# Two transformer blocks on one core: nearly half of the large expert-weight loads move from SyncE's queue to ScalarE's

## The reference, cut to what matters

```
def expert_block(args):
    xb, e = args
    hb = jax.nn.silu(xb @ w1[e]) * (xb @ w3[e])
    return hb @ w2[e]
```

## Time and profile before

| | us |
|---|---|
| median of 3 runs | 1780.15 (1780.12 to 1780.4) |
| the profiled execution, its own time | 1782.1 |
| span of the profiled execution on the core | 1780.8 |
| experts of layer 0 in the span | about 135 to 563 |
| experts of layer 1 in the span | about 677 to 1105 |

### The profile page before, as it was taken

One profiled execution on the slowest core, in us unless ns is written; L12 is line 12 of the kernel. 1 busy time (PEld: TensorE's weight loads), 2 busy tenths in 40 slices (PEclk: granted clock), 3 DMA queues, 4 the chain that ended last, 5 costly groups with the idle time before them and its releaser, 6 DMA issues.

```text
span 1780.8 us, 24002 instructions
## 1 busy us (share of the span) xinstructions
PE 1715.7 (96%) x10024; PEld 1119.8 (63%) x10024; DVE 790.6 (44%) x1510; ACT 624.1 (35%) x1197; POOL 120.7 (7%) x143
## 2 busy tenths in 40 slices
PE   9999999999999989999999989999999999999998
PEld 8974344433334974444333333887999898789986
DVE  6961111111103782111111012866888677668875
ACT  5541111000003661000000002666666564756664
POOL 0000000000000000000000000131111001401100
PEclk9999999999999999999999999999999999999999
DMA  9669999999999779999999999533555544435550
GB/s 389 239 246 409 421 428 428 427 429 426 427 424 419 277 300 394 409 430 429 426 428 428 426 425 419 182 127 134 183 182 190 189 166 146 139 128 174 185 189 24
DMA packets 55940, 544.90 MB, mean 306 GB/s; under 512 B 6288, under 2 KB 6288, under 8 KB 8336
## 3 DMA queue, kind: packets, MB, share of 16 engines
q1 hardware_dynamic: 55440, 542.14, 75.6%
q10 hardware_dynamic: 384, 1.13, 0.2%
HBM read 542.19 MB, written 1.05 MB: 305 GB/s over the span
## 4 chain that ended last, share of the span: by engine, by line
PE 69%; DMA 19%; DVE 7%; ACT 3%; issue 1%; POOL 1%; SPq 0%; DVEq 0%; ACTq 0%
PE PS L1136 24%; DMA ring<-in_w 19%; PE PS L407 12%; PE PS L409 11%; PE PS L408 11%; PE PS L1116 2%; DVE wl L390 2%; PE PS L1190 1%; PE PS L858 1%; PE PS L1152 1%; PE PS L617 1%; ACT wh L384 1%; PE PS L1204 1%; PE PS L1299 0%; DVE F L993 0%
## 5 line engine op out<-in xcount | busy, mean ns | idle before, releaser
L1136 PE MATMUL PS<-ring,F 128*64 128x512 f32 x2080 | 464.8, 597 | 26.7 <-DMA ring<-in_w 21.8
L390 DVE TENSOR_TENSOR wl<-ring,wh 128x512 fp32r<-128x512 f32 x504 | 363.3, 739 | 167.1 <-ACT wh L384 164.6
L384 ACT ACTIVATE wh<-ring 128x512 fp32r<-128x512 f32 x504 | 314.6, 631 | 272.0 <-PE PS L409 258.6
L1136 PEld LDWEIGHTS PS<-ring,F 128*64 128x64 f32 x2080 | 147.2, 137 | 321.1 <-issue 283.8
L407 PE MATMUL PS<-xh,wl 128*128 128x256 f32 x1168 | 336.5, 288 | 2.4 <-DVE wl L390 2.3
L408 PE MATMUL PS<-xl,wh 128*128 128x256 f32 x1168 | 330.3, 283 | 0.0
L409 PE MATMUL PS<-xh,wh 128*128 128x256 f32 x1168 | 330.3, 283 | 0.0
L407 PEld LDWEIGHTS PS<-xh,wl 128*128 128x128 f32 x1168 | 223.9, 192 | 5.6 <-DVE wl L390 2.6
L408 PEld LDWEIGHTS PS<-xl,wh 128*128 128x128 f32 x1168 | 223.9, 192 | 0.7
L409 PEld LDWEIGHTS PS<-xh,wh 128*128 128x128 f32 x1168 | 223.9, 192 | 0.0
L407 PE MATMUL PS<-wh,xl 128*128 128x512 f32 x352 | 142.6, 405 | 6.4 <-DVE xl L524 3.4
(11 more groups left out here) (391 smaller groups left out, 1881.4 us busy)
## 6 DMA issues: line engine op xcount, KB each, us to landing
ring<-in_w SPq DMA_DIRECT2D x100, 2048.0 KB, 25.6
ring<-in_w SPq DMA_DIRECT2D x66, 1024.0 KB, 10.5
ring<-in_ffn_up SPq DMA_DIRECT2D x44, 1024.0 KB, 4.9
early<-in_w SPq DMA_DIRECT2D x16, 2048.0 KB, 27.0
F<-in_w SPq DMA_DIRECT2D x16, 2048.0 KB, 29.2
ring<-in_ffn_down SPq DMA_DIRECT2D x22, 1024.0 KB, 4.9
F<-in_w SPq DMA_DIRECT2D x21, 1024.0 KB, 8.1
ZX<-in_w SPq DMA_DIRECT2D x8, 2048.0 KB, 26.9
```

The lines of the kernel that those rows point to most:

```text
L384: act.e.activation(self.wh[:, p % NPIECE, :], self.piece_source(p), ACT.Copy).then_inc(*self.up("w_hi", p))
L390: dve.e.tensor_tensor(self.wl[:, p % NPIECE, :], self.piece_source(p), f32(self.wh[:, p % NPIECE, :]), ALU.subtract).then_inc(*self.up("w_ ...
L1136: t = pe.e.matmul(PS[64 * half:64 * half + 64, bank, :], lhs(k), weights[:, a:a + 512], start=(k == 0), stop=(k == 7))
```

## The change

`_scalar_loads` picks the double loads for ScalarE: those for which the later of the two slots' former chunks is the last quarter of a matrix (`last % 4 == 3`). That is 30 of the 70 double loads of layer 0 (chunks 44, 64, 68, 72 and so on by four to 136, then 142, 146 and so on to 178), and 31 of layer 1 (60, 64 and so on to 124, then 130, 134, 136, 138, 142, 146 and so on to 178). SyncE leaves these out. ScalarE issues each one right after its operation that follows the product which used that last quarter: after the tanh (product with w1), after the copy of the turned hidden values (w3), or after the upper half of the result (w2). The slots, the sizes, the addresses and the signals are those of before.

```
+def _scalar_loads():
+    made = {}
+    for layer in range(2):
+        m = CHUNK[f"moe{layer}"]
+        for n in range(m, m + 192):
+            if FIRST_OF[n] == n and SIZE[n] == 2 and PREVIOUS[n + 1] >= m:
+                last = max(PREVIOUS[n], PREVIOUS[n + 1]) - m
+                if last % 4 == 3:
+                    made[n] = (layer, last // 12, last // 4 % 3)
+    return made
+BY_SCALAR = _scalar_loads()
...
     def sync_load(self, first, last):
-            if FIRST_OF[n] != n:
+            if FIRST_OF[n] != n or n in BY_SCALAR:
                 continue
...
+    def scalar_loads(self, layer, ex, w):
+        act = self.act
+        for n, after in BY_SCALAR.items():
+            if after == (layer, ex, w):
+                act.wait_ge(self.released(PREVIOUS[n]), self.released(PREVIOUS[n + 1]))
+                act.e.dma_start(self.chunk(n, 2), self.source(n)).then_inc(self.ring_sems[SLOT[n]], 16)
...
     def moe_scalar(self, layer, first, last):
             act.e.activation(v["hh"], PS[:, 4, :], ACT.Tanh, scale=0.5).then_inc(*up("tanh", layer, ex))
+            self.scalar_loads(layer, ex, 0)
...
             act.e.activation(v["hT"], PS[:, 4, :], ACT.Copy).then_inc(*up("hid_t", layer, ex))
+            self.scalar_loads(layer, ex, 1)
...
             act.e.activation(v["Y"][o][0:64, :], PS[0:64, 5, :], ACT.Copy).then_inc(*up("y0", layer, ex))
+            self.scalar_loads(layer, ex, 2)
```

## The result

The changed kernel takes 1788.9 us (median of 4, 1785.87 to 1791.31) against 1780.28 us (1780.12 to 1781.84) of before on the same chip: ratio 1.0043, 95% interval 1.0031 to 1.0055, so slower; the two medians are 8.6 us apart. On another chip it took 1790.42 against 1781.1 us, ratio 1.0052 (1.0038 to 1.0065). The profiled execution took 1786.99 us with a span of 1785.7, 4.9 us over before's span. Before's profiled execution was itself 1.8 us over its median (1782.1 against 1780.28), so lateness read between two profiles comes out that much smaller than the difference of the medians.

The account below looks back on a forecast made before the run. The prediction took the DMA transfers to set the pace until TensorE is work-bound at each layer's end. Terms 0 + 0 + 0 + 3.0 + 3.2 = 6.2 us on the 1780.15 us median gave 1786.3 us, range 1776 to 1797.

Parts of the forecast that it names:

- The bound, SyncE and ScalarE: Experts of both layers: loads run at one rate throughout; SyncE's 61 fewer issues and ScalarE's 61 issues each change 0.
- The rate with two queues: Weight loads in the experts: two queues move no more than one, 0; bounds 1% less and 1.9% more.
- faster rival: Weight loads: two queues hide what one leaves between packets, as in a 436 GB/s window; 6.9 us faster, 1773.3; chance 14%.
- The order of landing: End of each layer's experts: SyncE's chunk 172 lands only when all bytes up to 175 are in; 3.0 and 3.2 us.
- so the lead persists: ScalarE's loads land early: Experts' loads: each queue gets one load in two at half rate, so ScalarE's wait in their slots and SyncE's arrive last.
- layer 1's 3.2 us: End of layer 1's experts: chunks 172 to 175 run after 1062.16 in 7.1 us against 3.65, less 0.28 of waiting.
- the upper bound's case: End of each layer: ScalarE's 178 too gets ahead of SyncE's 172, another 4.9 us, up to 7.9 us a layer.

Follow-up runs that it names:

- one_packet: Kernel before, all real loads SyncE's; ScalarE issues 61 extra 8-byte one-packet loads, each waiting only for the third before it: 1781.07 against 1780.73 us, ratio 1.0.
- after_look: The changed kernel profiled once more, without any edit: 1791.2 us.
- the four profiles: Four profiled executions of the unedited changed kernel: 1786.99, 1788.63, 1791.2 and 1786.74 us.
- first profile: The first profiled execution of the changed kernel, without any edit: 1786.99 us.
- layer1_only: Changed kernel with ScalarE issuing its 31 loads in layer 1 alone, layer 0 as before the change: 1783.99 us, ratio 1.0016.
- last_three_only: Changed kernel with ScalarE issuing only chunks 170, 174 and 178 of each layer, six loads in all: 1796.24 against 1781.32 us, ratio 1.0082.
- other_half: Changed kernel with ScalarE and SyncE swapping halves (172 and 176 ScalarE's), issued ahead of ScalarE's next operation: 1787.63 against 1781.32 us, ratio 1.0035.
- last_three_back: Changed kernel with 170, 174 and 178 of each layer given back to SyncE, 55 loads still ScalarE's: 1781.63 against 1780.73 us, ratio 1.0005.

## Why the prediction was right

*The bound, SyncE and ScalarE.* All three held: the rate stayed at 428 and 426 GB/s, SyncE's share was 0, and ScalarE's 61 issues took 334 ns each and cost nothing (`one_packet`, ratio 1.0). The earlier trace rows is headed as SyncE's longest waits, but those at L365 for VectorE come to more (709.8 us in 118). That does not touch the argument, for it too is time in which SyncE had nothing to do.

*The rate with two queues.* The earlier trace rows had shown packets of both queues in turn and 425 GB/s in all; the 16 KB packets of the change do the same (1472 against 1467 between 250 and 350 us). From 200 to 350 us the rate was 428 GB/s with both queues at work. The faster rival's 436 is best read as the chance of a short window: in `after_look` two such windows next to each other have 421 and 411. The Trainium skill (DMA: Bandwidth & Descriptors, Issuing engines are not separate DMA queues) says that starting DMAs from several engines saves only the time to issue them, and this case agrees that no rate is won. By that rule alone the time would have stayed the same, and the measured ratio of 1.0043 decides against that.

*The order of landing.* That the loss lies in what lands when at each layer's end is shown, not only argued: without the last ten loads a layer nothing is lost (`not_the_tail`), with the last three alone 14.9 us are, and giving these three back leaves 0.9. In layer 0 the path was right too: 172 landed at 518.2 to 521.6 in the four profiles (forecast 519.64), chunks 172 to 175 ran in one piece, and only work was behind it.

*What was wrong in it.* The step "so the lead persists: ScalarE's loads land early" fails at the end of a layer. In the first profile's layer 0, ScalarE's loads landed 13 us ahead of the SyncE load before them from chunk 64 to 116, and 3.4 to 4.9 us ahead from 142 to 174. In layer 1, from 142 on, they landed 2.8 to 7.8 us behind it in all four profiles. So layer 1's 3.2 us was got by a step that did not happen: there it is ScalarE's own 174 that is late, by 2.5 us in `layer1_only`, and a fall of the clock adds 1.7. That 3.2 agrees with the 2.9 of that run is partly luck. By the prediction's own sign of being wrong, that ScalarE's loads do not land ahead of SyncE's, it failed in layer 1.

*Its size.* In the first profile 172 landed at 521.03 and not at 519.64. ScalarE's 178 was moving as well from 517.4 on, so part of it may have gone ahead, the upper bound's case in small. Layer 0 cost 4.26 in place of 3.0 in that profile and 3.8 alone. The sum of 6.2 us compares with 8.6 and 9.3 measured, 6.6 of it in the layers one by one. The term that was missing is the clock after a wait, 1.5 to 1.7 us where it comes.

*What it said of the profile.* Right: the rate, the queues' shares between 250 and 350 us, issue to landing apart there (27.9 against 45.4 us), the piece of 7.09 us in layer 0. Wrong in detail: it gave ScalarE's loads 10 to 25 us, and they took 13.7 to 32.1. It had TensorE's first wait for a load 10 to 40 us before 395.6; in before that wait had ended at 390.8, and in after it ended at 323.6. And the waits are longer, but hardly fewer. TensorE's waits for loads between 120 and 565 us, in after:

```profile
PE PS L1152 <- DMA ring<-in_w: 15.7, 8, 2.7
PE PS L1152 <- DMA F<-in_w: 2.5, 1, 2.5
```

and in before:

```profile
PE PS L1136 <- DMA ring<-in_w: 7.9, 9, 1.3
PE PS L1136 <- DMA F<-in_w: 2.7, 1, 2.7
```

Nine against ten, but 18.2 us against 10.6.

*Open:* why both layers together cost 2 to 2.7 us more than one by one (within the intervals), why the queues stand differently at the end of the two layers, and what sets whether an execution comes at 1786 or 1791. The granted clock was 0.993 to 0.996 in the four runs up to 1787.03 us and 0.992 to 0.994 in the seven above, which goes the same way but shows no cause.

## What to carry to other kernels

When transfers are the bound and one queue is never empty, as here, a second queue moves no more bytes in sum; it only changes which load is complete when. That costs what the needed load is late at the last place where the consumer has no more slack, and cost nothing elsewhere here, so look there and not at the number of loads moved. A load put on an empty queue beside one that is five deep jumps the line. If loads must be split over queues, keep the last ones before such a place in one queue: that brought the loss down to 0.9 us and to nothing here, while every way that split them to the end of both layers cost 3.4 to 14.9 us.

## What the runs showed of the hardware

- Fewer moved loads cost more: 6 loads 14.9 us, 61 loads 8.6. In `last_three_only` ScalarE's loads took 15.1 us to land and SyncE's 172 took 35.5, both of 2 MB, 172 issued 4.9 us after ScalarE's 170.
- A load of 1 KB in 128 packets needs 9.2 us beside a full queue. Each of the 16 engines has 8 of its packets, and if each waits for one packet of the other queue (4.9 us / 8 = 0.61), that is 4.9 us of the 9.2; this is an estimate, and the rest is open. The Trainium skill (DMA: Bandwidth & Descriptors, Queues, rings and completion order) says that an engine changes queues only at packet boundaries; the trace agrees with its 1472 packets against 1467.
- Packets of 8 bytes are not free: 3867 packets with 0.03 MB took 0.7% of the 16 engines over 300 us, some 9 ns each (an estimate from these numbers), and moved the end of layer 0 by 2.5 us.
- A wait of TensorE was followed in several profiles by a stretch at 1.2 GHz that made 16 matmuls take 5.2 to 5.35 us in place of 3.65: waits of 2.62, 2.93 and 3.75 us in the changed kernel's layer 1, 2.02 us in `other_half` (523.13), 2.74 us in before (402.01, 5.27 us). A wait of 2.73 us in the first profile of after (521.17) was not, its 32 matmuls took 7.09. The length of the wait alone does not tell these apart.
- What such a fall costs depends on the place: `last_three_back` had a mean granted clock of 0.993 to 0.996 against 0.996 to 0.999 in before on the same chip, and lost 0.9 us.
